# Modulation tiles taken out of the recurrence's twelve steps and set whole in front of steps 28 to 37

## The reference

```python
mod = silu(cond) @ w_mod + b_mod                   # cond: c for latent rows, c_ctx for context rows; 6 x 2048 columns
sh_m, sc_m, g_m, sh_f, sc_f, g_f = split(mod, 6)
h = rmsnorm(x, norm_g[0]) * (1 + sc_m) + sh_m
u = h @ w_in                                       # 5120 columns: heads A, B, C, D
# A differential attention, B bidirectional RG-LRU (conv, gates, two scans), C neighbourhood, D grouped attention
x = x + g_m * rmsnorm(concat(A, B, C, D) @ w_out, norm_g[1])
h = rmsnorm(x, norm_g[2]) * (1 + sc_f) + sh_f
x = x + g_f * rmsnorm((silu(g) * a) @ w_ffn_out, norm_g[3])    # a, g = split(h @ w_ffn_in)
```

## Time and profile before

| | us |
|---|---|
| median of 3 runs (lowest, highest) | 1812.4 (1811.48, 1816.27) |
| profiled execution | 1815.88 |
| its span | 1813.9 |
| TensorE busy in it | 1768.0 (97%) |
| VectorE, ScalarE, GpSimd busy | 944.8, 658.6, 126.6 |
| mean DMA rate over the span | 175 GB/s |

### The profile page before, as it was taken

How to read it: one execution, slowest core, us unless ns; L and a number is a source line. 1 busy time by engine, 2 the same in 40 slices (tenths; PEclk the granted TensorE clock), 3 DMA queues, 4 the chain that set the end, 5 groups by cost and what they waited for, 6 DMA issues and landing times.

```text
span 1813.9 us, 22196 instructions
## 1 busy us (share of the span) xinstructions
PE 1768.0 (97%) x9277; PEld 1518.8 (84%) x9277; DVE 944.8 (52%) x1268; ACT 658.6 (36%) x951; POOL 126.6 (7%) x172
## 2 busy tenths in 40 slices
PE   4999999999999999999999999999999999999998
PEld 1677666677778879999999999999999988888886
DVE  4455467732556678355566543333333455555554
ACT  3432253433464434222222222222222345454442
POOL 1000124450300002000000000000000000000000
PEclk9999999999999999999999999999999999999999
DMA  9877776675422241445454543333333333333331
GB/s 372 328 305 300 302 266 264 258 300 225 159 105 93 93 186 52 181 147 201 186 196 175 204 145 124 132 120 135 117 139 117 138 117 131 125 122 134 119 114 70
DMA packets 46907, 317.32 MB, mean 175 GB/s; under 512 B 5468, under 2 KB 7912, under 8 KB 9752
## 3 DMA queue, kind: packets, MB, share of 16 engines
q1 hardware_dynamic: 44192, 302.14, 44.5%
q0 software_dynamic: 2288, 10.56, 1.7%
q10 hardware_dynamic: 328, 3.21, 0.5%
HBM read 310.50 MB, written 5.39 MB: 174 GB/s over the span
## 4 chain that ended last, share of the span: by engine, by line
PE 95%; DVE 2%; DMA 1%; issue 1%; POOL 0%; ACT 0%; SPq 0%; DVEq 0%; POOLq 0%
PE ps L1077 40%; PE ps L856 9%; PE ps L858 8%; PE ps L857 8%; PE ps L770 6%; PE ps L769 6%; PE ps L768 6%; PE ps L747 4%; DMA raw<-in_weights 1%; PE ps L967 1%; PE ps L990 1%; PE ps L917 1%; PE ps L1025 1%; PE ps L980 1%; PE ps L756 0%
## 5 line engine op out<-in xcount | busy, mean ns | idle before, releaser
L1143 DVE TENSOR_TENSOR wlo<-raw,whi 128x1024 fp32r<-128x1024 f32 x376 | 458.6, 1233 | 706.8 <-ACT whi L424 706.8
L424 ACT ACTIVATE whi<-raw 128x1024 fp32r<-128x1024 f32 x376 | 392.3, 1058 | 848.3 <-PE ps L1077 507.0
L1077 PE MATMUL ps<-h_hi,whi 128*128 128x384 f32 x1408 | 471.4, 335 | 0.5 <-DVE h_lo L1227 0.5
L1077 PE MATMUL ps<-h_hi,wlo 128*128 128x384 f32 x1408 | 470.4, 334 | 0.0
L1077 PE MATMUL ps<-h_lo,whi 128*128 128x384 f32 x1408 | 470.3, 334 | 0.0
L856 PE MATMUL ps<-whi,h_hi 128*128 128x512 f32 x660 | 274.5, 416 | 0.7 <-DVE h_lo L1260 0.5
L1077 PEld LDWEIGHTS ps<-h_hi,whi 128*128 128x128 f32 x1408 | 264.3, 188 | 0.7 <-issue 0.7
L1077 PEld LDWEIGHTS ps<-h_lo,whi 128*128 128x128 f32 x1408 | 264.3, 188 | 0.0
L1077 PEld LDWEIGHTS ps<-h_hi,wlo 128*128 128x128 f32 x1408 | 264.3, 188 | 0.0
L858 PE MATMUL ps<-wlo,h_hi 128*128 128x512 f32 x660 | 258.6, 392 | 0.0
L857 PE MATMUL ps<-whi,h_lo 128*128 128x512 f32 x660 | 257.6, 390 | 0.0
(11 more groups left out here) (254 smaller groups left out, 1213.4 us busy)
## 6 DMA issues: line engine op xcount, KB each, us to landing
raw<-in_weights SPq DMA_DIRECT2D x284, 1024.0 KB, 4.9
xT<-in_x_t ACTq DMA_DIRECT2D x1, 3072.0 KB, 12.6
out<-x_sb SPq DMA_DIRECT2D x6, 512.0 KB, 2.7
x_sb<-in_x_sample POOLq DMA_DIRECT2D x1, 2048.0 KB, 10.7
sbc<-silu_rows POOLq DMA_DIRECT2D x1, 2048.0 KB, 10.8
gw<-in_lru_gate_w SPq DMA_DIRECT2D x4, 256.0 KB, 2.9
out<-U POOLq DMA_DIRECT2D x4, 256.0 KB, 5.7
nabias<-rpb_pad POOLq DMA_DIRECT2D x16, 64.0 KB, 3.3
```

The source lines that it names most:

```text
L424: nc.scalar.activation(whi[:, 2 * (g % RING) + b], raw[:, t % RAW, HK * b:HK * b + HK].rearrange("p k n -> p (k n)"), ACT.Copy).then_inc(w ...
L1077: return nc.tensor.matmul(ps[bank][:, 0:T], w[:, k % KH * P:(k % KH + 1) * P], xs[:, k, :], start=first, stop=last)
L1143: V.tensor_tensor(wlo[:, 2 * (t % RAW) + b], raw[:, t % RAW, HK * b:HK * b + HK].rearrange("p k n -> p (k n)"), whi[:, 2 * (g % RING) + b] ...
```

## The change

The function that says which modulation tiles stand in front of a step is the only one touched:

```diff
 def mod_tiles(s):

-    m, first = 2 + s // 2, s % 2 * 2
-    if s == 0 or m >= len(MOD_ORDER):
+    if EARLY * KG + 12 <= s < EARLY * KG + 22:
+        return s - 18, [0, 1, 2, 3]
+    if s == 0 or s >= EARLY * KG:
         return 0, []
-    return m, [0, 1, 2, 3] if s == 1 else [first, first + 1]
+    return 2 + s // 2, [0, 1, 2, 3] if s == 1 else [s % 2 * 2, s % 2 * 2 + 1]
```

## The result

| | before | after |
|---|---|---|
| median us (lowest, highest; runs) | 1814.34 (1811.48, 1817.75; 4) | 1893.05 (1891.78, 1901.22; 4) |
| span of the profiled execution | 1813.9 | 1889.9 |
| TensorE busy | 1768.0 | 1784.0 |
| mean granted clock | 0.996 | 0.977 |

The change makes the kernel 4.4% slower: ratio 1.0443, 95% interval 1.0406 to 1.0479. Forecast were 1871 us and a range up to 1892; the direction was right, the time lies 22 us above the forecast and 1 us outside the range.

What follows compares the result with a forecast made beforehand. TensorE's work plus its idle time was taken as the bound (busy 1768.0 of 1813.9 us). -30 + 24.8 + 52 + 12 = +58.8 on 1815.88 gave 1874.7, less 3.5 for the median: 1871 us, range 1844 to 1892.

Steps and rivals of the forecast that it cites:

- The recurrence, -30: Steps 16 to 27: 24.8 us of tiles and turns leave, 7.2 of waits and low clock go, 2 of new waits come.
- The moved work, +24.8: Steps 28 to 37: the 24 modulation tiles and 6 turns that leave steps 16 to 27 come back here, +24.8 us.
- The stops, +52: Steps 28 to 36: late weight tile holds up ScalarE's and VectorE's queues, TensorE stops once per step; 52 us in all.
- lands 4.7 + 4 x 2.48 = 14.6 us after the end of the matmuls: Attention steps: the weight tile, last of five loads, lands after 4.7 us for the first and 2.48 for each other.
- M + 13.9: M is the start of a step's modulation tiles; ScalarE was to wait at the weight tile's split until 13.9 us later.
- the 53.4 reckoned: Sum in us of the nine stops forecast for steps 28 to 36, taken as 52.
- The clock, +12: Low clock behind the nine stops at 1.6 us each, 14.6 us, of which 12 were taken.
- Hidden loads: Rival: in steps 28 to 37 weight tiles land before M + 8 and nothing stops; -5.2 us, 1807 us, chance 0.08.
- No low clock: Rival: TensorE stops as forecast, but without the 12 us of low clock; 1859 us, chance 0.11.
- half the stop: Rival: stops of 3 us in nine steps, 27 instead of 52, and half the low clocks; 1840 us, chance 0.09.
- VectorE binding the recurrence: Rival: scans and splits push the gates back 3 us in three rounds, recurrence term -21; 1880 us, chance 0.08.
- Slower loads: Rival: loads in the attention steps take 2 us more in each of nine steps; 1889 us, chance 0.08.

Runs made afterwards that it cites:

- one load of four: Changed kernel, but of each of modulation groups 10 to 19 only the first of four tiles is loaded and read four times; 1807.85 us, ratio 0.9969.

## Why the prediction was wrong in size

- *The recurrence, -30.* Measured -29.1. The parts held in kind: no wait for loads, VectorE even with TensorE. In size the new waits were 4.3 us with 1.7 of low clock, where I allowed 2. What made up for them is busy time, which fell by 27.8 us (140.81 - 113.00) where 24.8 + 1.6 - 1.7 = 24.7 would follow; these 3 us aren't explained, so that the sum came out within 0.9 us is in part luck.
- *The moved work, +24.8.* Held: with one load of four, and so without stops, busy time is 148.78 us, where 125.39 + 24.8 is 150.2.
- *The stops, +52.* This is the first term that failed. The mechanism, the nine steps and the work that TensorE stands in front of are those of the forecast, the size was 60.7. The failed step is "lands 4.7 + 4 x 2.48 = 14.6 us after the end of the matmuls": in steps 31 to 36 the split began 14.7 to 16.8 us after it. Only steps 32 and 33 keep to the reckoning. In place of M + 13.9 (13.8 where it is worked out; the terms give 13.7 to 14.1) the measured starts in steps 28 to 36 are 17.7, 17.0, 14.3, 15.6, 13.6, 13.5, 14.8, 16.2 and 16.1 us, 15.4 in the mean. I took the best rate and the shortest landing that the trace had shown for all five loads, as if nothing else used the DMA engines, although rows 8 had a median of 6.3 and a longest of 9.4 against 4.7. The rate had little part in it: in the middle of step 32's loads the engines moved 427 GB/s, and 395 in step 31's, against the 423 of rows 7. Against the 53.4 reckoned, steps 28 and 29 (8.4, with the short wait of 1.2, and 6.2 for 4.5 and 3.9) and 35 and 36 (9.1 and 9.7 for 6.6 and 8.0) make 10.4 of the excess; the five others give 1.5 back, though no split of theirs but those of steps 32 and 33 came early. Most of that is step 30, where TensorE was late as well: behind step 29's stop its four modulation tiles took 6.4 us at the low clock instead of 3.6, it reached its second gap at M + 13.8 instead of M + 10.8, and stood for 4.4 instead of 6.0. Rounding 53.4 down to 52 went the wrong way too.
- *The clock, +12.* The second. 18.8 us in busy time. A low stretch followed each of the nine stops, not eight out of ten, and cost 2.1 us of busy time each and not 1.6, which had come from the single low stretch of the earlier trace rows. The rule of the Trainium skill that I weighed ("TensorE: Matmul & The Clock Gate", section "HAM oscillation — how this bites in real kernels"), that every tile then starts on a clock that has fallen, held at nine stops of nine. For short idle times the length doesn't decide in these traces: 1.95 and 1.71 us were followed by a low clock, 2.62 and 1.53 us were not, nor was a third idle time in the recurrence before, of 1.08 us, which the prediction left out.
- *The rivals.* Hidden loads: wrong, unless the queues are reordered. No low clock, half the stop: wrong. VectorE binding the recurrence: not to that degree, 4.3 us of waits and not 9. Slower loads, 0.08 for 1889, was the nearest to the measured 1893 and right in kind: the splits came 1.5 us later than reckoned in the mean, for its 2. It was near in number in part by luck, since the stops made up 8.7 us of the excess, not 18, and the clock another 6.8. It stood as a case apart; it should have moved the forecast itself, since nothing in the trace said that loads ever land earlier than the best.
- *The range.* Two errors of the same sign, 8.7 and 6.8 us, with the recurrence's 0.9, make 16.4 of the 22. Outside these steps the spans differ by another 0.9, the medians differ by 78.7 us where the spans differ by 76.0, and I built on 1812.4, the median of three runs, where that of all four is 1814.34. Both terms could only be wrong upwards, and a range of +21 over -27 did not say so.

## What to carry to other kernels

When tiles are moved in a stream of loads with a short ring, ask of each step which load is now the last to be issued behind a buffer's release, and which in-order queue takes it up first; all that stands behind that wait is late, however small, and the list of waits will name the small thing. A load that fits the bandwidth of a step can still be too late for its queue. The cheap cure is to put the work that others wait for ahead of the wait, not to move the loads: that gave back 68 us here, and 3.6 us on the kernel as it was. A longer ring, or the weight tile's load ahead of the step's modulation loads, might do the same; neither was tried.

## What was not expected of the hardware

- The last of five loads issued together landed late: in steps 31 to 36 the split began 14.7 to 16.8 us after the end of the matmuls, against 4.7 + 4 x 2.48 = 14.6, and the late steps are the same in two profiles. GpSimd's DMAs explain part of it in steps 29 and 36; in steps 31 and 35 one packet of the instruction queue lies among the loads in both profiles, which no run took away. The cause there stays open.
- Behind each stop of 4.4 to 9.7 us the clock was at 1.2 GHz for a while, and filling the stops of seven steps with useless matmuls made the kernel 10 us faster.
